# The two squared-ReLU MLPs without r in the relu: ScalarE takes the relu, and r squared becomes a per-token column in the additions of the down products

## What is computed

```python
def _rmsnorm(x, g):
    xf = x.astype(jnp.float32)
    y = xf * lax.rsqrt(jnp.mean(xf * xf, axis=-1, keepdims=True) + EPS)
    return (y * g.astype(jnp.float32)).astype(x.dtype)

def _sqrelu_mlp(h, w1, w2):
    u = jax.nn.relu(h @ w1)
    return (u * u) @ w2

...
    h = h + _sqrelu_mlp(_rmsnorm(h, mlp_norm_g[i]), mlp_w1[i], mlp_w2[i])
return _rmsnorm(h, final_norm_g)
```

## Time and profile before

| | us |
|---|---|
| runs (3): median | 1966.59 |
| lowest to highest | 1965.65 to 1966.99 |
| the profiled execution | 1966.46 |
| its span in the trace | 1964.7 |

### The profile page before, as it was taken

The page is one execution under the profiler, slowest core; times in us unless marked ns, Lnnn a source line. Parts: engine busy times, 40 slices in busy tenths (PEclk is TensorE's granted clock), DMA queues, the critical chain, the costliest instruction groups (busy, mean ns, idle before and its releaser), DMA issues.

```text
span 1964.7 us, 23668 instructions
## 1 busy us (share of the span) xinstructions
PE 1940.4 (99%) x9216; PEld 1609.4 (82%) x9216; DVE 1205.0 (61%) x1703; ACT 882.3 (45%) x1286; POOL 604.4 (31%) x442
## 2 busy tenths in 40 slices
PE   8999999999999999999999999999999999999998
PEld 6777878888888888888888888888888888888886
DVE  6657663332257854545455857668566676766757
ACT  7445543322234552525255534434455555444435
POOL 2333645454555335353533000000333341000000
PEclk9999999999999999999999999999999999999999
DMA  5312367276222313232225557374322226736553
GB/s 164 94 44 76 97 98 115 93 122 116 89 86 86 128 65 107 65 101 69 96 76 150 150 156 186 108 191 110 106 85 85 85 65 182 189 112 171 128 172 86
DMA packets 166339, 221.31 MB, mean 113 GB/s; under 512 B 4641, under 2 KB 120097, under 8 KB 166113
## 3 DMA queue, kind: packets, MB, share of 16 engines
q1 hardware_dynamic: 151728, 190.52, 29.8%
q0 software_dynamic: 12928, 25.71, 7.6%
q10 hardware_dynamic: 1584, 3.74, 4.3%
HBM read 214.84 MB, written 4.72 MB: 112 GB/s over the span
## 4 chain that ended last, share of the span: by engine, by line
PE 84%; DVE 5%; ACT 3%; issue 3%; DMA 2%; POOL 1%; SPq 0%; DVEq 0%; ACTq 0%; POOLq 0%
PE ps L921 27%; PE ps L923 26%; PE ps L922 26%; DMA aux<-in_mlp_w 2%; POOL w_lo L815 1%; PE ps L1093 1%; PE ps L1123 1%; ACT w_hi L1626 1%; DVE o_buf L3065 1%; PE ps L1132 1%; PE ps L1133 1%; PE ps L1110 1%; ACT w_hi L1608 0%; DVE w_lo L3004 0%; DVE aux L3056 0%
## 5 line engine op out<-in xcount | busy, mean ns | idle before, releaser
L815 POOL TENSOR_TENSOR w_lo<-raw,w_hi 128x512 fp32r<-128x512 f32 x376 | 531.2, 1444 | 668.8 <-ACT w_hi L1608 668.8
L921 PE MATMUL ps<-hn_hi,w_hi 128*128 128x512 f32 x1524 | 602.4, 395 | 4.7 <-POOL w_lo L815 2.8
L923 PE MATMUL ps<-hn_hi,w_lo 128*128 128x512 f32 x1524 | 594.1, 390 | 0.0
L922 PE MATMUL ps<-hn_lo,w_hi 128*128 128x512 f32 x1524 | 593.9, 390 | 0.0
L921 PEld LDWEIGHTS ps<-hn_hi,w_hi 128*128 128x128 f32 x1524 | 286.4, 188 | 68.8 <-POOL w_lo L815 3.8
L923 PEld LDWEIGHTS ps<-hn_hi,w_lo 128*128 128x128 f32 x1524 | 286.3, 188 | 60.7
L922 PEld LDWEIGHTS ps<-hn_lo,w_hi 128*128 128x128 f32 x1524 | 286.6, 188 | 58.9 <-issue 1.7
L1608 ACT ACTIVATE w_hi<-raw 128x2048 fp32r<-128x2048 f32 (+1 forms) x98 | 186.1, 1899 | 286.7 <-PE ps L923 286.6
L1626 ACT ACTIVATE w_hi<-raw 128x1024 fp32r<-128x1024 f32 x112 | 116.2, 1056 | 208.2 <-PE ps L923 208.0
L921 PE MATMUL ps<-w_hi,hid_hi 128*128 128x512 f32 x456 | 178.5, 391 | 2.4 <-DVE o_buf L3065 2.2
L922 PE MATMUL ps<-w_lo,hid_hi 128*128 128x512 f32 x456 | 177.5, 389 | 0.0
(11 more groups left out here) (356 smaller groups left out, 2852.8 us busy)
## 6 DMA issues: line engine op xcount, KB each, us to landing
raw<-in_mlp_w SPq DMA_DIRECT2D x56, 1024.0 KB, 5.4
raw<-in_ret_w_in SPq DMA_DIRECT2D x24, 1024.0 KB, 5.1
aux<-in_mlp_w POOLq DMA_DIRECT2D x16, 1024.0 KB, 9.0
raw<-in_att_w_in SPq DMA_DIRECT2D x12, 1024.0 KB, 5.6
raw<-in_w_gate SPq DMA_DIRECT2D x11, 1024.0 KB, 5.4
raw<-in_w_up SPq DMA_DIRECT2D x11, 1024.0 KB, 5.3
raw<-in_w_down SPq DMA_DIRECT2D x8, 1024.0 KB, 8.1
raw<-in_ret_w_out SPq DMA_DIRECT2D x8, 1024.0 KB, 5.1
```

Source lines behind the costliest of these rows:

```text
L815: ins = pool.tensor_tensor(w_lo[:, slot, at], raw[:, slot, at], w_hi[:, slot, at].bitcast(F32), ALU.subtract)
L921: pe.matmul(o, hi, rhs_hi, start=start, stop=False, skip_group_check=True)
L922: pe.matmul(o, hi, rhs_lo, start=False, stop=False, skip_group_check=True)
L923: return pe.matmul(o, lo, rhs_hi, start=False, stop=stop, skip_group_check=True)
```

## The change

- ACT does the relu, from PSUM straight into `u_squared` and without r, and then squares in place. DVE's `relu` is gone. Relu and square raise the same semaphores as before.
- The statistic of both MLPs is taken by `stat_columns`, in bank 7, at k = 3; DVE's two operations on the halves, the two 512-column matmuls and ACT's two 512-column operations are gone. ACT makes r squared (`r_for_tokens`: Ln, Exp with scale -1, and a copy with the sign turned) as columns of the new tile `r_two`: four for plus, four for minus, one per 128 tokens.
- `take` is one operation for each bank, product times column plus x. A double addition becomes two operations of 128x512, a single one keeps its shape. A subtraction uses the columns of minus.

```diff
-N_MLPA = Norm(N_RET, 8, 8, halves=True)
+N_MLPA = Norm(N_RET, 8, 8, columns=True)
 N_ATT = Norm(N_MLPA, 0, 8, by_tokens=True)
-N_MLPB = Norm(N_ATT, 8, 8, halves=True)
+N_MLPB = Norm(N_ATT, 8, 8, columns=True)
...
+        r_two = sb("r_two", [P, 8])
...
-            def stat_columns(norm):
+            def stat_columns(norm, bank=6):
...
-                    ins = pe.matmul(ps[:, 6, t:t + 1], ssq[:, t * P:(t + 1) * P], ones[:, 0:1], start=True, stop=True)
+                    ins = pe.matmul(ps[:, bank, t:t + 1], ssq[:, t * P:(t + 1) * P], ones[:, 0:1], start=True, stop=True)
...
                     if k >= 4:
                         to_tokens(kept, k - 4)
-                    if 3 <= k < 5:
-                        stat_halves(norm, k - 3)
+                    if k == 3:
+                        stat_columns(norm, 7)
...
+                def r_for_tokens():
+
+                    act.wait_ge(s["col_stat"], 2 + ml.layer)
+                    act.activation(r_two[:, 0:4], ps[:, 7, 0:4], ACT.Ln, scale=1.0 / D, bias=eps[:, 0:1])\
+                        .then_inc(s["col_ln"], 1)
+                    act.wait_ge(s["col_ln"], 2 * ml.layer + 2)
+                    act.activation(r_two[:, 0:4], r_two[:, 0:4], ACT.Exp, scale=-1.0).then_inc(s["mlp_r"], 1)
+                    act.wait_ge(s["mlp_r"], 2 * ml.layer + 1)
+                    act.activation(r_two[:, 4:8], r_two[:, 0:4], ACT.Copy, scale=-1.0).then_inc(s["mlp_r"], 1)
+
                 def squared(g, m):
 
-                    act.wait_ge(s["mlp_up_taken"], ml.ups(g, m))
+                    bank, u = (Y, X)[m % 2], u_squared[:, 2 * m:2 * m + 2, :]
+                    act.wait_ge(s["group_done"], ml.done(g, m, 1))
                     if g == 0:
                         act.wait_ge(s["x_t"], turned + 2 * m + 2)
-                    act.activation(u_squared[:, 2 * m:2 * m + 2, :], sq, ACT.Square).then_inc(s["mlp_sq"], 1)
+                    act.activation(u, ps[:, bank:bank + 2, :], ACT.Relu).then_inc(s["mlp_up_taken"], 1)
+                    act.wait_ge(s["mlp_up_taken"], ml.ups(g, m))
+                    act.activation(u, u, ACT.Square).then_inc(s["mlp_sq"], 1)
...
                         if g == 0 and m == 0:
-                            rsqrt(norm, D)
+                            r_for_tokens()
                             for f in range(4):
                                 token_copy(f)
                         squared(g, m)
...
-                def relu(g, m):
-
-                    bank = (Y, X)[m % 2]
-                    dve.wait_ge(s["group_done"], ml.done(g, m, 1))
-                    if ml.ups(g, m) > 1:
-                        dve.wait_ge(s["mlp_sq"], ml.ups(g, m) - 1)
-                    dve.scalar_tensor_tensor(sq, ps[:, bank:bank + 2, :], 0.0, r_bc.unsqueeze(1).to_broadcast([P, 2, S]),
-                                             ALU.max, ALU.mult).then_inc(s["mlp_up_taken"], 1)
-
...
-                    o = token_block(f, t)[:, tiles, :]
-                    dve.tensor_tensor(o, o, ps[:, bank + tiles.start:bank + tiles.stop, :], op).then_inc(s["mlp_taken"], 1)
-
-                dve.wait_ge(s["norm_r"], norm.index + 1)
+                    for n in range(tiles.start, tiles.stop):
+                        o, at = token_block(f, t)[:, n, :], 2 * t + n + (0 if op is ALU.add else 4)
+                        ins = dve.scalar_tensor_tensor(o, ps[:, bank + n, :], r_two[:, at:at + 1], o, ALU.mult, ALU.add)
+                    ins.then_inc(s["mlp_taken"], 1)
+
...
-                        relu(g, m)
```

More of the change, by code:

```diff
@@ L257, with __init__ @@
 class Norm:
-    def __init__(self, prev, n, split, halves=False, by_tokens=False):
+    def __init__(self, prev, n, split, halves=False, by_tokens=False, columns=False):
         self.n, self.split, self.halves = n, split, halves
         self.added = 0 if by_tokens else n + 1 if halves else n - 1
-        self.index = prev.index + (not by_tokens) if prev else 0
+        self.index = prev.index + (not by_tokens and not columns) if prev else 0
         self.sq0 = prev.sq0 + prev.n if prev else 0
@@ L298 @@
  gain_pair old_hi old_lo apart_done apart_scaled apart_sum gate_old_done gate_e_hi gate_e_lo gate_sig gate_read
- mlp_up_taken mlp_sq mlp_sum mlp_hi mlp_lo mlp_taken s3_in s3_added a21_in s1_added m_summed s4_added
+ mlp_up_taken mlp_r mlp_sq mlp_sum mlp_hi mlp_lo mlp_taken s3_in s3_added a21_in s1_added m_summed s4_added
  att_in_hi att_in_lo tab_scaled ffn_silu ffn_part token_sq token_sum r_diagonal r_spread r_row fin_weighed fin_left fin_right""".split()
@@ L1652, in rsqrt_columns @@
                     .then_inc(s["col_ln"], 1)
-                act.wait_ge(s["col_ln"], nth + 1)
+                act.wait_ge(s["col_ln"], 2 * nth + 1)
                 act.activation(r_col[:, 0:4], r_col[:, 0:4], ACT.Exp, scale=-0.5).then_inc(s["col_r"], 1)
@@ L2323, in token_rsqrt @@
                     .then_inc(s["col_ln"], 1)
-                act.wait_ge(s["col_ln"], 3 + t)
+                act.wait_ge(s["col_ln"], 5 + t)
                 act.activation(r_col[:, t:t + 1], r_col[:, t:t + 1], ACT.Exp, scale=-0.5).then_inc(s["col_r"], 1)
@@ L3096, in mlp @@
                         dve.wait_ge(s["x_copied"], kept + KD)
+                        dve.wait_ge(s["mlp_r"], 2 * ml.layer + 2)
                     half_lo(ml, g, ml.M, 0)
```

## The result

The changed kernel takes 1973.98 us (median of 5 runs, 1972.82 to 1975.23), the kernel before 1966.59 us (5 runs on the same chip, 1965.2 to 1967.31): 1.0037 times as long, with a 95% interval of 1.0024 to 1.005. It is slower by some 7.4 us. The profiled execution took 1974.42 us, its span 1972.6 us: 7.96 and 7.9 us more than those of before.

The account below looks back on a forecast made before the run. PE, busy 99%, was taken as the bound, with a slackless chain through DVE's additions pacing S4. Terms 5.0 + 0.2 + 0.9 + 1.0 + 0.2 = 7.3 us on 1966.46 us gave 1973.8 us, range 1968.6 to 1976.4.

Parts of the forecast that it names:

- Additions, +5.0 us: DVE's chain to S4: Q1, Q2, Q4 +0.19 us each, Q5 +0.06; 0.63 us a group, eight groups.
- The lower bound (1.7 us): Same chain if the column costs nothing and the two operations overlap: +0.07 us a double, 0 a single.
- Relu: Relu moved to ACT: PE waits 0.45 us at each MLP's third up product, +0.9 us; other groups +0.2 us.
- The 0.2 us for the six other groups: ACT's relu between splits delays S3's first half; some 0.05 us gets through per group, +0.2 us (0 to 1.5).
- Statistic, +1.0 us: On PE, four one-column products replace two of 512 columns: +0.49 us an MLP, range 0 to 1.9 us.
- Ends, +0.2 us: At each MLP's end, one or two single additions behind PE's last matmul, 0.06 us longer each.
- the free split: Q1, Q2, Q4 on DVE: two halves run nearly as close as one whole; 1968.8 us, no change; chance 0.16.
- the late ACT: Relu and square in a row on ACT ahead of S3 make it late: +2.4 us, 1976.2 us; chance 0.10.
- the shortening DVE: DVE, freed of relu, shortens the chain to S4: 1963.3 us if all 5.5 us of waits went; chance 0.04.

Follow-up runs that it names:

- reordered kernels: Kernel before and changed kernel, each with Q5's first half ahead of Q2 and Q4 on DVE: 1964.51 us and 1965.76 us.
- the column alone: Kernel before with each addition as one operation per bank with a column of plus or minus one; relu and statistic as before: 1972.58 us against 1966.74 us.
- relu on DVE: Changed kernel with all relus back on DVE, times one, split additions and column statistic kept: 1971.76 us, 1.0032 of the kernel before.

## Why the prediction was right, by its steps

- **Additions, +5.0 us: right, in size and place.** The double went from 1.22 to 1.40 us, Q5 to 0.75; the chain grew by 0.63 us in the first group and its legs by 0.18 and 0.44 in the others; S4's delays by 5.1 us. The reordered kernels show that nearly all of the price is paid in front of S4. The lower bound (1.7 us) was the price of two operations without a column, measured at 1.4 us. The row of line 3142 was the right one to take, since it has the same form. The Trainium skill (VectorE: DVE Perf Modes, The DRAIN you can't avoid) has each vector operation followed by a flush, by which each second operation would pay in full, and lets one that isn't held start earlier; the plain pair cost 0.07 us where 683 ns twice without overlap is 0.15 us more than 1.22, so the trace agrees with the second and not with the first.
- **Relu: the wait right, the rest nothing.** The wait was forecast at 0.45 us and is 0.43 in both MLPs. Relu takes 1.01 us from PSUM, a little less than the 1.05 taken. The 0.2 us for the six other groups did not come: ACT's wait for PE ahead of S3's second half took relu in, with 0.76 us to spare. (Six times the 0.05 us would be 0.3 in any case, and with relu at 1.20 some 1.2 in place of 1.5; neither moves the forecast.)
- **Statistic, +1.0 us: right.** 0.47 us in each MLP by the difference of PE's starts; the one-column products took 0.80 us in place of 0.85.
- **Ends, +0.2 us: right at the second MLP, nothing at the first.** Behind PE's last matmul 0.15 us is added, 0.07 for each of two additions. At the end of the first MLP the difference of PE's starts stays as S4 left it.
- **Not in the prediction:** the clock at the attention, +1.6 us in this execution, 0.5 us that come off behind it, and 0.3 us the other way ahead of the first MLP. They make up the gap between the terms as measured (7.1 us) and the span's 7.9. That the median lies within 0.2 us of the forecast is therefore in part luck: the fall may come in more of the changed kernel's runs (all five have a mean clock of 0.998, which leaves room for it) than in those of before (34 of the 67 on record have 0.999, which leaves none), and the median would then hold part of its 1.6 us, which the sum of the prediction does not have. The mechanism rests on the traces and the reordered kernels, not on that agreement.
- **The rivals:** the free split fell with the column alone (+5.8 us); the late ACT and the shortening DVE with relu on DVE, whose legs are the same.

## What to carry to other kernels

Before an instruction is made longer, ask which chain it stands in: here 0.19 us, three times in each of eight groups, on an engine that is idle 39% of the time cost 5 us, since the work stood in front of the one that frees PE's bank. Such a chain is often only the order of a queue: putting the addition that frees the bank ahead of two that free nothing yet removed the wait altogether, and with it nearly all of the price of the split. It took away no more than PE's wait: the end of the program, which followed DVE's row of additions, came only 1.1 us earlier where PE's last matmul came 2.1 us earlier. To part such a change from the scatter, split the chain into legs between fixed instructions; in like groups they repeated within 0.02 us where the runs scatter by 3.

## What the runs showed of the hardware that had not been expected

- A 128x512 operation of the form product times column plus x takes 745 ns where the plain addition of PSUM takes 683: the column's form costs 62 ns. Two in a row on different banks overlap by 0.09 us (1.40 in place of 1.49).
- The time from issue to the landing of the same accumulating transfer goes from 8.2 to 10.1 us over the groups and kernels, and each 0.1 us of it is 0.1 us of PE as long as the chain has no slack. In the three profiles of the kernel before S4's delays are 3.4, 2.6 and 2.3 us; from the first to the second the eight landings are together 0.8 us shorter, and the delays 0.8 us.
- The granted clock can fall to 0.5 (1.2 GHz) for some 3 us behind a PE wait of 2.4 us, and does so in some executions of the same program only; it costs 1.5 to 1.6 us. What decides it stays open.
